# One item of the inverse split in two, and the gates' exponents listed as items of their own

## The chip, the cores and the metric

The kernel runs on one core of one Trainium2 chip. The metric is the device time of one execution in microseconds. The engines of the core are named as in the profile: PE (TensorE, matmuls), PEld (its weight loads), DVE (VectorE), ACT (ScalarE), POOL (GpSimd) and SP (SyncE, whose queue issues most DMAs). Each engine works through its own instructions in order and waits on semaphores for the others.

## The reference

Two layers of a hybrid block over 256 context and 256 latent tokens of width 1024, all in f32. Each layer norms and modulates its input, projects it, and feeds three mixers: a gated linear attention, a gated DeltaNet in both directions, and a latent attention. Their outputs are gated, projected, merged and projected again. What the change touches is the DeltaNet, and in it the inverse of a unit lower triangular matrix per chunk and head, and the sigmoid gates of the merge:

```python
l_strict = jnp.where(strict, jnp.einsum('bnthd,bnshd->bnhts', k_beta, k) * decay, 0.0)
t_inv = lax.linalg.triangular_solve(eye + l_strict, jnp.broadcast_to(eye, l_strict.shape),
                                    left_side=True, lower=True, unit_diagonal=True)
u = jnp.einsum('bnhts,bnshv->bnthv', t_inv, v_beta)
w = jnp.einsum('bnhts,bnshd->bnthd', t_inv, k_beta * jnp.exp(g_cum)[..., None])
...
def step(s, inp):
    w_n, u_n, qd_n, att_n, ke_n, d_n = inp
    v_new = u_n - jnp.einsum('bthd,bhdv->bthv', w_n, s)
    o_n = jnp.einsum('bthd,bhdv->bthv', qd_n, s) + jnp.einsum('bhts,bshv->bthv', att_n, v_new)
    s = s * d_n[..., None, None] + jnp.einsum('bshd,bshv->bhdv', ke_n, v_new)
...
def merge_branches(ya, yb, yc, gate_logits, w_branch, w_out):
    ys = jnp.einsum('btiw,iwd->btid', jnp.stack([ya, yb, yc], axis=2), w_branch)
    gates = jax.nn.sigmoid(gate_logits.reshape(B, T, N_BRANCH, D_MODEL))
    return jnp.einsum('btd,de->bte', jnp.sum(gates * ys, axis=2), w_out)
```

## The kernel before

The whole program is one list, made by `schedule()`. An entry is an item such as `("dw", l, g)`: a kind, the layer `l` (0 or 1) and further indices. Every engine walks the same list and for each item issues the instructions that are its part, so an item may have matmuls on PE, then a function on ACT and a product on DVE, with semaphores between. The order of the list is the order on each engine. The list is put together from shorter ones: `weave` merges several of them so that each progresses evenly by the sum of its items' loads (1.0 for most, 0.3 for a few light kinds), and `settle` at the end moves kinds by a fixed number of places (table `AHEAD`; for `gx` it is -4, four places later, for `dx6`, `dya` and `dy6` 3 and for `dyb` 2 places earlier; `dw` has no entry). An item more in one of the woven lists therefore also moves its neighbours. Long matmul groups are cut in quarter pieces (`("pc", ...)`), between which other items may stand. Eight PSUM banks and four slots of weights (`ring`) are handed out along the list; PE waits for a bank's readers and for its weights.

The DeltaNet's heads are taken in four groups of two (`g`). The items of a group:

- `dqkv`, `cv`, `dsilu`, `dsil2`, `dnq`, `dn`: projection, convolution, silu (three functions on ACT, L1471 to L1473, for `dsilu`, an exponent for `dsil2`, L1690) and norm of the next group's q, k, v.
- `d1`, `d2`, `dd`, `dt`: decays (an exponent on ACT, L1710), the products of keys, four copies of the diagonal blocks by ACT (L1723) and a small transpose by DVE (L2119), per token tile. SP then stores the blocks to DRAM.
- `sol`: POOL loads all blocks of 32 x 32 of the group (L1068), solves them, and lands the inverses in SBUF again (the last DMAs are issued on L1094).
- `dv`: DVE copies the landed blocks (L2140) and transposes them (L2143).
- `dw`: ACT sets the blocks in their places, four copies into `XN` (L1734) and eight into `bXT` (L1739), each with 32 partitions and 256 elements.
- `dx`, `dya`, `dyb`, `dx6`, `dy6`: PE joins the blocks to 64 and then 128; DVE takes `dx` (L2145), `dya` and `dx6` out of PSUM, ACT takes `dyb` (four copies, L1746), and both take `dy6` (L1751 on ACT). `dx6` reads `XN`, `dy6` and the scan read `bXT`.
- `d3`: transposed keys and values of a tile; ACT copies one half (L1716), DVE multiplies the other (L2127).
- `sk`, `sq`, `st`, `su`, `sa`: the four steps of the scan. `st` is copied by ACT (L1757) before `su` and `sa` may use it.

Gates come in the merge: `gate` (projection of a block of 128 columns, three functions on ACT, L1471 to L1473, and DVE's subtraction, which is the item with the mark `"v"`, L1934) and `ys` (projection of the branch). In `ys` ACT first takes the exponent of the gate (L1652), then DVE multiplies (L1948). For six blocks of the last layer the exponent is an item `gx` of its own already (L1646). The gates and `ys` pieces of branch 0 are woven as filling work around the inverses and scans; PE does the other matmuls of the list while the small chain runs.

Of the kernel before, what the change touches and what calls it, by code (L numbers as in the profile page):

```python
# [9 lines left out]
ACT = mybir.ActivationFunctionType  # L10
# [6 lines left out]
KT = D // P  # L17
# [155 lines left out]
def schedule():  # L173
# [31 lines left out]
    def merge(l, br):  # L205
        if keeps(("gate", l, br, 0)):
            out = [i for e in range(6, 8) for i in pieces(("gate", l, br, e)) + [("v", "gate", l, br, e)]]
            return out + [i for e in range(8) for i in pieces(("ys", l, br, e))]
        out = []
        for e in range(9):  # L210
# [3 lines left out]
            out += p[:2] + ([("v", "gate", l, br, e)] if e < 8 else []) + p[2:]  # L214
# [60 lines left out]
    def invert(l, g):  # L275

        return [(k, l, g) for k in ("dv", "dw", "dx", "dya", "dyb", "dx6", "dy6")]
# [85 lines left out]
    for l in range(DEPTH):  # L363
# [20 lines left out]
        if sums:  # L384
# [13 lines left out]
          "dv": "invert", "dw": "invert", "dx": "invert", "dya": "invert", "dyb": "invert", "dx6": "invert", "dy6": "invert",  # L398
# [4 lines left out]
         "dd": 0, "dt": 0, "sol": 0, "dv": 0, "dw": 0, "dg": 2}  # L403
# [61 lines left out]
def hybrid_block(nc, x, c, ctx_in, c_ctx, norm_w, ada_w, ada_b, w_in, gla_gate_w2, gla_gate_b, gla_norm_w,  # L465
# [55 lines left out]
    with ExitStack() as stack:  # L521
# [153 lines left out]
        def takes_part(it, who):  # L675
            return not (it[0] == "ys" and keeps(it) and who == "act")
# [77 lines left out]
        for key, its in phase_items.items():  # L754
            d = {}
            for it in its:
# [357 lines left out]
        def _(pe):  # L1114
# [10 lines left out]
            for it in plan:  # L1125
# [340 lines left out]
        def _(act):  # L1466
# [38 lines left out]
            for it in plan:  # L1505
# [135 lines left out]
                elif k == "gx":  # L1641
                    gi = ("gate",) + it[1:]
                    act.wait_ge(*done(gi, "dve"))
                    act.wait_ge(s_spill, 16 * (l + 1))
                    act.wait_ge(s_scaled, KT * (l + 1))
                    ins = nc.scalar.activation(yT[:, it[3], 0:LC], E1[:, zg_index[gi] % 2, LC:T], ACT.Exp)  # L1646
                elif k in ("z2", "ys"):

                    zi = ("z" if k == "z2" else "gate",) + it[1:]
                    act.wait_ge(*done(zi, "dve"))  # L1650
                    e = E1[:, zg_index[zi] % 2, (q0 if k == "ys" else 0):512]
# [675 lines left out]
```

## Time and profile before

| what | us |
|---|---|
| median of 3 runs | 2241.01 |
| lowest, highest | 2238.62, 2243.85 |
| profiled execution | 2241.74 |
| its span, first to last instruction | 2239.9 |
| PE busy | 2138.0 |
| DVE, ACT, POOL busy | 917.0, 846.1, 291.5 |

The page of the profile gives the busy time of every engine. A timeline row gives the start, the duration, the engine, the line, the operation with its operands and how many records were merged; in brackets stands the idle time in front and what ended it. A matmul in f32 has two records, a transpose through PE one.

### The profile page before, as it was taken

Reading aid. Unit: us, or ns where it says so; the run is one execution under the profiler, and the core shown is the slowest. Engines: PE = TensorE matmul, PEld = TensorE weight load, DVE = VectorE, ACT = ScalarE, POOL = GpSimd, SP = SyncE. Lnnn points to the kernel's source line nnn. Section 1 sums busy time; section 2 is a strip of 40 time slices with the busy share of each in tenths; the row PEclk is TensorE's granted clock in tenths of the full one; section 3 lists DMA queues with packets and bytes.
Section 4 is the critical chain, followed back from the end, with each engine's and each line's share of the span. In section 5 each row is a group of like instructions: output and inputs, shape, how many; then the busy total and the mean of one; then the engine's idle time right before and its main releaser. Section 6 shows DMA issues by size and latency. Waiting matters only on the chain. (4 is left out here: it accounts for less than half of the span.)

```text
span 2239.9 us, 31521 instructions
## 1 busy us (share of the span) xinstructions
PE 2138.0 (95%) x10970; PEld 1458.9 (65%) x10970; DVE 917.0 (41%) x2281; ACT 846.1 (38%) x2205; POOL 291.5 (13%) x623
## 2 busy tenths in 40 slices
PE   7999899999989999999999998999989979999998
PEld 4667576655555786555584445776666758877687
DVE  2023374657554325333331111136486654343321
ACT  2223263546343224444332102245455453244420
POOL 1000006061431000000000001000523532000000
PEclk9999999999999999999999999999999999999999
DMA  8324412221212122111321325221332222332333
GB/s 269 101 67 160 126 41 78 79 60 53 85 34 67 29 66 87 48 38 40 95 75 57 119 74 171 59 76 39 95 95 86 72 62 87 102 106 70 123 116 130
DMA packets 192444, 192.32 MB, mean 86 GB/s; under 512 B 28943, under 2 KB 186467, under 8 KB 191779
## 3 DMA queue, kind: packets, MB, share of 16 engines
q1 hardware_dynamic: 186048, 171.08, 24.7%
q0 software_dynamic: 4672, 18.89, 2.7%
q8 instruction: 93, 1.52, 0.3%
q10 hardware_dynamic: 1571, 0.34, 0.1%
q14 instruction: 60, 0.49, 0.1%
HBM read 180.78 MB, written 9.50 MB: 85 GB/s over the span
## 5 line engine op out<-in xcount | busy, mean ns | idle before, releaser
L1118 PE MATMUL bank<-hT,ring 128*128 128x512 f32 (+2 forms) x1856 | 721.1, 539 | 3.6 <-DVE hT L1882 2.1
L1118 PEld LDWEIGHTS bank<-hT,ring 128*128 128x128 f32 (+1 forms) x1856 | 333.1, 190 | 257.9 <-issue 240.5
L1118 PE MATMUL bank<-ring,hT 128*128 128x256 f32 (+2 forms) x2112 | 455.2, 371 | 12.6 <-DMA ring<-in_w_in_dram 12.6
L1118 PEld LDWEIGHTS bank<-ring,hT 128*128 128x128 f32 x2112 | 383.9, 192 | 77.2 <-issue 30.2
L1118 PE MATMUL bank<-WORK 128*128 128x128 f32 (+6 forms) x3056 | 393.0, 286 | 30.6 <-issue 8.7
L1118 PEld LDWEIGHTS bank<-WORK 128*128 128x128 f32 (+4 forms) x3056 | 320.9, 171 | 134.7 <-issue 117.1
L1118 PE MATMUL bank<-yT,ring 128*128 128x512 f32 (+1 forms) x768 | 268.7, 487 | 0.0
L1118 PEld LDWEIGHTS bank<-yT,ring 128*128 128x128 f32 x768 | 138.8, 190 | 83.7 <-issue 75.4
L1471 ACT ACTIVATE E<-bank 128x512 f32<-128x512 f32 (+1 forms) x84 | 44.9, 535 | 254.0 <-PE bank L1118 253.8
L2068 DVE SCALAR_TENSOR_TENSOR WORK<-WORK,CW 128x512 f32<-128x512 f32 (+1 forms) x192 | 139.0, 724 | 2.3
L1118 PE MATMUL bank<-ring,WORK 128*128 128x384 f32 (+1 forms) x272 | 108.4, 536 | 0.0
L1081 POOL TENSOR_TENSOR WORK<-WORK 128x126 f32<-128x126 f32 (+22 forms) x248 | 104.5, 421 | 19.4
L1106 POOL DMA_DIRECT2D yT<-xs x2 | 1.1, 548 | 809.4 <-DVE MT L1952 809.4
L1079 POOL TENSOR_TENSOR WORK<-WORK 128x126 f32<-128x126 f32 (+22 forms) x248 | 101.4, 409 | 19.5
L1483 ACT ACTIVATE WORK<-bank 128x128 f32<-128x128 f32 (+3 forms) x182 | 47.3, 272 | 134.3 <-PE bank L1118 134.1
L1118 PE MATMUL bank<-MT,ring 128*128 128x512 f32 (+1 forms) x256 | 83.9, 486 | 2.7 <-DVE MT L1952 2.7
L1121 PEld LDWEIGHTS bank<-K,WORK 128*128 128x128 f32 (+1 forms) x506 | 63.5, 143 | 31.0 <-issue 23.3
L1121 PE MATMUL bank<-K,WORK 128*128 128x128 f32 (+1 forms) x506 | 81.5, 279 | 0.0
L1118 PEld LDWEIGHTS bank<-ring,WORK 128*128 128x128 f32 x272 | 50.3, 190 | 37.9 <-issue 22.0
L1118 PEld LDWEIGHTS bank<-MT,ring 128*128 128x128 f32 x256 | 48.5, 190 | 37.2 <-issue 30.1
L1676 ACT ACTIVATE WORK<-bank 128x512 f32<-128x512 f32 (+1 forms) x48 | 26.9, 560 | 105.5 <-PE bank L1118 105.5
L1970 DVE SCALAR_TENSOR_TENSOR WORK<-bank,WORK 128x512 f32<-128x512 f32 x16 | 11.1, 692 | 126.9 <-ACT WORK L1473 126.9
(208 smaller groups left out, 2088.9 us busy)
## 6 DMA issues: line engine op xcount, KB each, us to landing
ring<-in_w_in_dram SPq DMA_DIRECT2D x92, 1024.0 KB, 5.4
ring<-in_w_branch_dram SPq DMA_DIRECT2D x24, 1024.0 KB, 5.1
ring<-in_ada_w_dram SPq DMA_DIRECT2D x18, 1024.0 KB, 5.6
ring<-in_w_out_dram SPq DMA_DIRECT2D x8, 1024.0 KB, 5.0
WORK<-in_ada_w_dram SPq DMA_DIRECT2D x6, 1024.0 KB, 12.3
ring<-in_mla_q_up_dram SPq DMA_DIRECT2D x8, 576.0 KB, 4.3
xs<-yT POOLq DMA_DIRECT2D x2, 2048.0 KB, 8.1
WORK<-LD POOLq DMA_DIRECT2D x16, 256.0 KB, 3.5
```

The costliest lines, as they stand in the source:

```text
L1079: link(pool, "pool", pool.tensor_tensor(t, a[:, j + 1:BASE, j:j + 1].broadcast_to([P, m, w]), y[:, j:j + 1, 0:w].broadcast_to([P, m, w]), ...
L1081: ins = pool.tensor_tensor(y[:, j + 1:BASE, 0:w], y[:, j + 1:BASE, 0:w], t, ALU.subtract)
L1106: pool.dma_start(yT[:, :, :], xs[l]).then_inc(s_back, 16)
L1118: return nc.tensor.matmul(o, a, b, start=start, stop=stop, skip_group_check=True)
L1121: return nc.tensor.transpose(o, a, ident)
L1471: link(act, "act", nc.scalar.activation(dst, src, ACT.Abs))
L1483: ins = nc.scalar.activation(MT2[:, c0:c0 + w], ps[:, c0:c0 + w], ACT.Square, accum_out=mS[:, at + i:at + i + 1])
L1676: ins = nc.scalar.activation(PAD[:, 2 * pj + a0:2 * pj + 2, 2:258], ps[:, a0 * LC:T].rearrange("p (s n) -> p s n", n=LC), ACT.Copy)
L1970: ins = V_.scalar_tensor_tensor(LA[:, tt, :], ps[:, :], 0.0, LT1, ALU.min, ALU.subtract)
L2068: ins = V_.scalar_tensor_tensor(acc, src, wv, acc, ALU.mult, ALU.add)
```

## The change

The eight copies into `bXT` leave `dw` and are a new item `dw2`, listed directly behind `dx`. `dx6` still waits for `dw`; `dy6` (on PE and DVE) waits for `dw2`, as do the next group's `dv` and the first readers of group 3's scan. The wait for the scan of the group before moves from `dw` to `dw2` and `dyb`.

Every gate gets an item `gx`, listed directly behind its `"v"` item, and takes its exponent there. `ys` has no part on ACT any more.

```diff
     def merge(l, br):
         if keeps(("gate", l, br, 0)):
-            out = [i for e in range(6, 8) for i in pieces(("gate", l, br, e)) + [("v", "gate", l, br, e)]]
+            out = [i for e in range(6, 8) for i in pieces(("gate", l, br, e)) + [("v", "gate", l, br, e), ("gx", l, br, e)]]
...
-            out += p[:2] + ([("v", "gate", l, br, e)] if e < 8 else []) + p[2:]
+            out += p[:2] + ([("v", "gate", l, br, e), ("gx", l, br, e)] if e < 8 else []) + p[2:]
...
     def invert(l, g):
-        return [(k, l, g) for k in ("dv", "dw", "dx", "dya", "dyb", "dx6", "dy6")]
+        return [(k, l, g) for k in ("dv", "dw", "dx", "dw2", "dya", "dyb", "dx6", "dy6")]
...
         def takes_part(it, who):
-            return not (it[0] == "ys" and keeps(it) and who == "act")
+            return not (it[0] == "ys" and who == "act")
...
                     pe.wait_ge(*done(("dx6", l, g), "dve"))
                     pe.wait_ge(*done(("dyb", l, g), "act"))
+                    pe.wait_ge(*done(("dw2", l, g), "act"))
...
                 elif k == "gx":
                     gi = ("gate",) + it[1:]
                     act.wait_ge(*done(gi, "dve"))
-                    act.wait_ge(s_spill, 16 * (l + 1))
-                    act.wait_ge(s_scaled, KT * (l + 1))
-                    ins = nc.scalar.activation(yT[:, it[3], 0:LC], E1[:, zg_index[gi] % 2, LC:T], ACT.Exp)
-                elif k in ("z2", "ys"):
+                    if keeps(gi):
+                        act.wait_ge(s_spill, 16 * (l + 1))
+                        act.wait_ge(s_scaled, KT * (l + 1))
+                        ins = nc.scalar.activation(yT[:, it[3], 0:LC], E1[:, zg_index[gi] % 2, LC:T], ACT.Exp)
+                    else:
+                        e = E1[:, zg_index[gi] % 2, q0:512]
+                        ins = nc.scalar.activation(e, e, ACT.Exp)
+                elif k == "z2":
...
                 elif k == "dw":
                     _, l, g = it
                     act.wait_ge(*done(("dv", l, g), "dve"))
+                    if g:
+                        act.wait_ge(*done(("dx6", l, g - 1), "pe"))
+                    for b in range(NBLK):
+                        half = slice(0, 2 * BASE) if b < 2 else slice(2 * BASE, 4 * BASE)
+                        ins = nc.scalar.activation(two_heads(XN)[blk(b), :, :, blk(b % 2)],
+                                             two_heads((LAND if b < 2 else LANDT)[:, :, half])[blk(b)], ACT.Copy)
+                elif k == "dw2":
+                    _, l, g = it
+                    act.wait_ge(*done(("dv", l, g), "dve"))
                     act.wait_ge(s_zero, 4 * l + 4)
                     if g:
                         scan_left(act, l, g - 1, NB - 1, "pe")
-                        act.wait_ge(*done(("dx6", l, g - 1), "pe"))
-                    for b in range(NBLK):
...
                     for b in range(NBLK):
                         for r in range(2):
...
                 elif k == "dyb":
                     _, l, g = it
+                    if g:
+                        scan_left(act, l, g - 1, NB - 1, "pe")
...
                     e = E1[:, zg_index[gi] % 2, q0:512]
+                    dve.wait_ge(*done(("gx",) + it[1:], "act"))
                     if keeps(it):
-                        dve.wait_ge(*done(("gx",) + it[1:], "act"))
                         e = yT[:, e8, 0:LC]
-                    else:
-                        dve.wait_ge(*done(it, "act"))
...
```

The order on ACT in layer 1 around the inverse of group 2, before. L1716 is a copy of `d3`, the four copies on L1734 and the eight on L1739 are `dw`, and L1652 is the exponent of a gate.

```order
L1716 ACTIVATE WORK<-bank 128x256
L1734 ACTIVATE O<-WORK 32x4x2x32 x2
L1734 ACTIVATE O<-O 32x4x2x32 x2
L1739 ACTIVATE WORK<-O 32x4x2x32
L1739 ACTIVATE WORK<-WORK 32x4x2x32
L1739 ACTIVATE WORK<-O 32x4x2x32
L1739 ACTIVATE WORK<-WORK 32x4x2x32
L1739 ACTIVATE WORK<-O 32x4x2x32
L1739 ACTIVATE WORK<-WORK 32x4x2x32
L1739 ACTIVATE WORK<-O 32x4x2x32
L1739 ACTIVATE WORK<-WORK 32x4x2x32
L1652 ACTIVATE E<-E 128x256
```

The same place of ACT in the changed kernel. L1714 is the exponent of `d1`, L1651 that of the gate, L1727 the copies of `dd`, L1720 `d3`, L1736 `dw` and L1747 the beginning of `dw2`.

```order
L1714 ACTIVATE SQ<-SQ 128x512 x2
L1651 ACTIVATE E<-E 128x256
L1727 ACTIVATE WORK<-SQ 32x128 x8
L1720 ACTIVATE WORK<-bank 128x256
L1736 ACTIVATE O<-WORK 32x4x2x32 x2
L1736 ACTIVATE O<-O 32x4x2x32 x2
L1720 ACTIVATE WORK<-bank 128x256
L1747 ACTIVATE WORK<-O 32x4x2x32
L1747 ACTIVATE WORK<-WORK 32x4x2x32
```

The exponent has moved from behind the twelve copies to before the last two `dd`, and one more `d3` copy has come between the four and the eight.

The order on ACT in layer 1 behind the inverse of group 1, before. L1471 to L1473 with `WORK` are the functions of `dsilu`, with `E` those of a gate; L1676 is a projection's copy, L1690 `dsil2`, and L1757 the copy of the first `st`.

```order
L1471 ACTIVATE WORK<-WORK 128x512
L1472 ACTIVATE WORK<-WORK 128x512
L1473 ACTIVATE WORK<-WORK 128x512
L1676 ACTIVATE WORK<-bank 128x256
L1690 ACTIVATE WORK<-WORK 128x512
L1471 ACTIVATE E<-bank 128x256
L1472 ACTIVATE E<-E 128x256
L1473 ACTIVATE E<-E 128x256
L1757 ACTIVATE WORK<-bank 128x512
L1471 ACTIVATE WORK<-WORK 128x512
L1472 ACTIVATE WORK<-WORK 128x512
L1473 ACTIVATE WORK<-WORK 128x512
```

The same place of ACT in the changed kernel, where every line number is a little higher (L1472 to L1474, L1680, L1694, and L1767 for `st`).

```order
L1472 ACTIVATE E<-bank 128x256
L1473 ACTIVATE E<-E 128x256
L1474 ACTIVATE E<-E 128x256
L1472 ACTIVATE WORK<-WORK 128x512
L1473 ACTIVATE WORK<-WORK 128x512
L1474 ACTIVATE WORK<-WORK 128x512
L1680 ACTIVATE WORK<-bank 128x256
L1694 ACTIVATE WORK<-WORK 128x512
L1472 ACTIVATE WORK<-WORK 128x512
L1473 ACTIVATE WORK<-WORK 128x512
L1474 ACTIVATE WORK<-WORK 128x512
L1767 ACTIVATE WORK<-bank 128x512
```

The gate's functions have moved ahead of the first `dsilu`, and the second `dsilu` ahead of the copy of `st`.

The order on PE in layer 1 from the last `dn` of group 3 (`RS`) to the first matmuls of `dx` of group 2 (32x32), before. `hT` rows are quarter pieces of gates, `yT` rows pieces of `ys`, `K,WORK` 128x128 x8 two `d1`, and `WORK` 128x128 rows are `d2`.

```order
L1118 MATMUL bank<-RS,ONES 128x512
L1118 MATMUL bank<-K,WORK 128x128 x8
L1118 MATMUL bank<-hT,ring 128x256 x2
L1118 MATMUL bank<-WORK 128x128 x4
L1118 MATMUL bank<-hT,ring 128x256 x2
L1118 MATMUL bank<-K,WORK 128x128 x8
L1118 MATMUL bank<-yT,ring 128x256 x2
L1118 MATMUL bank<-WORK 128x128 x8
L1118 MATMUL bank<-yT,ring 128x256 x4
L1121 MATMUL bank<-K,WORK 128x128 x4
L1118 MATMUL bank<-yT,ring 128x256 x2
L1118 MATMUL bank<-WORK 32x32 x2
```

The same place of PE in the changed kernel.

```order
L1118 MATMUL bank<-RS,ONES 128x512
L1118 MATMUL bank<-K,WORK 128x128 x8
L1118 MATMUL bank<-yT,ring 128x256 x2
L1118 MATMUL bank<-WORK 128x128 x4
L1118 MATMUL bank<-yT,ring 128x256 x2
L1118 MATMUL bank<-K,WORK 128x128 x8
L1118 MATMUL bank<-WORK 128x128 x8
L1118 MATMUL bank<-yT,ring 128x256 x4
L1118 MATMUL bank<-hT,ring 128x256 x2
L1121 MATMUL bank<-K,WORK 128x128 x4
L1118 MATMUL bank<-hT,ring 128x256 x2
L1118 MATMUL bank<-WORK 32x32 x2
```

The two gate pieces (`hT`) that stood behind the `dn` have gone ahead of it, into the scan of group 1, and two pieces of the next gate stand ahead of `dx` instead.

## Rows read from the trace of the kernel before

**Rows 1.** The page: the span, and busy time, share and instructions of each engine

```profile
span 2239.9 us, 31521 instructions
PE 2138.0 (95%) x10970; PEld 1458.9 (65%) x10970; DVE 917.0 (41%) x2281; ACT 846.1 (38%) x2205; POOL 291.5 (13%) x623
```

**Rows 2.** Waits of PE: total us, times, longest

```profile
PE bank L1118 <- DVE WORK L2145: 9.7, 4, 5.1
```

**Rows 3.** Timeline of PE, layer 1, group 2: start, us, operation, count [idle before]

```profile
1821.11 0.18 PE L1118 MATMUL bank<-WORK 32*32 32x32 f32 x1 [4.17 <-DVE O L2143]
...
1827.04 0.23 PE L1118 MATMUL bank<-WORK,O 32*32 32x32 f32 x1 [5.10 <-DVE WORK L2145]
...
1828.95 3.54 PE L1118 MATMUL bank<-hT,ring 128*128 128x256 f32 x8
...
1867.73 3.62 PE L1118 MATMUL bank<-hT,ring 128*128 128x256 f32 x16
```

**Rows 4.** Timelines of ACT and DVE at the same place

```profile
1825.63 0.42 ACT L1652 ACTIVATE E<-E 128x256 f32<-128x256 f32 x1
...
1826.13 0.42 DVE L1948 TENSOR_TENSOR MT<-bank,E 128x256 f32<-128x256 f32 x1 [4.54 <-issue]
1826.47 0.41 DVE L2145 COPY WORK<-bank 128x256 f32<-128x256 f32 x1
```

**Rows 5.** Timelines of DVE, POOL and PE: the solve of layer 1, group 3

```profile
1819.14 0.24 DVE L2119 STREAM_TRANSPOSE WORK<-WORK 128x64 f32<-128x64 f32 x1 [1.18 <-ACT WORK L1723]
...
1821.77 0.54 POOL L1068 DMA_DIRECT2D WORK<-LD  x1 [28.22 <-DMA LD<-WORK]
...
1869.33 0.43 DVE L2140 COPY WORK<-WORK 128x512 f32<-128x512 f32 x1 [1.88 <-DMA WORK<-XD]
...
1871.28 0.21 PE L1118 MATMUL bank<-WORK 32*32 32x32 f32 x1
```

**Rows 6.** Line L1739, copies of `dw`: ns least/median/most, first and last start

```profile
L1739 ACT ACTIVATE WORK<-O x32: 412/414/418, 435.5 to 1874.6; 32x256 f32<-32x256 f32 x32
```

**Rows 7.** Timelines of PE, DVE and ACT, layer 1, inverse and first scan step of group 1

```profile
1728.09 0.18 PE L1118 MATMUL bank<-WORK,O 32*32 32x32 f32 x1 [2.35 <-DVE WORK L2145]
...
1735.57 0.76 DVE L2127 TENSOR_TENSOR WORK<-bank,WORK 128x256 f32<-128x256 f32 x2 [0.22 <-ACT WORK L1716]
...
1737.99 1.52 ACT L1746 ACTIVATE WORK<-bank 32x256 f32<-32x256 f32 x4
...
1739.66 0.53 PE L1118 MATMUL bank<-WORK 64*64 64x64 f32 x11 [0.23 <-ACT WORK L1746]
...
1748.51 0.58 ACT L1757 ACTIVATE WORK<-bank 128x512 f32<-128x512 f32 x1
...
1749.19 1.13 PE L1118 MATMUL bank<-WORK 128*128 128x128 f32 x8 [1.23 <-issue]
```

**Rows 8.** Groups of ACT's instructions by line and shape: count, busy us, mean ns, idle before

```profile
L1472 ACT ACTIVATE WORK<-WORK 128x512 f32<-128x512 f32 x56 | 35.3, 630 | 1.8
```

**Rows 9.** Timelines of PE and DVE, layer 0

```profile
445.94 1.17 PE L1118 MATMUL bank<-WORK 64*64 64x64 f32 x32 [0.79 <-ACT WORK L1746]
...
642.71 0.23 PE L1118 MATMUL bank<-WORK 32*32 32x32 f32 x1 [4.42 <-DVE O L2143]
...
644.46 0.23 PE L1118 MATMUL bank<-WORK,O 32*32 32x32 f32 x1 [0.61 <-DVE WORK L2145]
...
676.10 2.02 PE L1118 MATMUL bank<-WORK 128*128 128x128 f32 x16 [1.27 <-DVE WORK L2163]
...
692.98 0.89 DVE L2143 STREAM_TRANSPOSE O<-WORK 128x128 f32<-128x128 f32 x4
...
697.38 0.21 PE L1118 MATMUL bank<-WORK 32*32 32x32 f32 x1
```

**Rows 10.** Busy time by stretch: us, engines (records), PE's granted clock, DMA share, GB/s

```profile
1822.00:1832.00 10.00, 4.96 (x44) 4.24 (x44) 2.35 (x6) 4.35 (x12) 6.09 (x14) 0.50 0.21 56
1400.00:1410.00 10.00, 10.00 (x48) 8.79 (x47) 0.69 (x1) 2.11 (x4) 0.00 (x0) 1.00 0.01 2
```

More of the change, by code:

```diff
@@ L397 @@
 FAMILY = {"d1": "head", "d2": "head", "dd": "head", "dt": "head", "d3": "head",
-          "dv": "invert", "dw": "invert", "dx": "invert", "dya": "invert", "dyb": "invert", "dx6": "invert", "dy6": "invert",
+          "dv": "invert", "dw": "invert", "dw2": "invert", "dx": "invert", "dya": "invert", "dyb": "invert", "dx6": "invert", "dy6": "invert",
           "sk": "scan", "sq": "scan", "st": "scan", "su": "scan", "sa": "scan"}
 NBANK = {"nx": 0, "nh": 0, "cv": 0, "dsilu": 0, "dsil2": 0, "dnq": 0, "osq": 0, "z2": 0, "gx": 0, "rstd": 0, "ge": 2, "mkv": 1,
-         "dd": 0, "dt": 0, "sol": 0, "dv": 0, "dw": 0, "dg": 2}
+         "dd": 0, "dt": 0, "sol": 0, "dv": 0, "dw": 0, "dw2": 0, "dg": 2}
 READERS = {"xin": ("act",), "par": ("act",), "mod": ("dve",), "modT": ("dve",), "norm": ("act",), "z": ("act", "dve"),
@@ L763, in hybrid_block @@
         NODVE = {"gx", "norm", "osq", "dqkv", "pc", "dnq", "xin", "gqk", "gv", "lr", "mp", "xout", "mkT",
-                 "dd", "sol", "dw", "dyb", "st"}
+                 "dd", "sol", "dw", "dw2", "dyb", "st"}
         POOLK = {"sol"}
@@ L768, in hybrid_block @@
                 continue
-            if k not in ("nx", "nh", "cv", "dsilu", "dsil2", "dnq", "osq", "z2", "gx", "rstd", "dd", "dt", "sol", "dv", "dw"):
+            if k not in ("nx", "nh", "cv", "dsilu", "dsil2", "dnq", "osq", "z2", "gx", "rstd", "dd", "dt", "sol", "dv", "dw", "dw2"):
                 parts["pe"].add(k)
@@ L1643, in _ @@
                     act.wait_ge(*done(gi, "dve"))
-                    act.wait_ge(s_spill, 16 * (l + 1))
-                    act.wait_ge(s_scaled, KT * (l + 1))
-                    ins = nc.scalar.activation(yT[:, it[3], 0:LC], E1[:, zg_index[gi] % 2, LC:T], ACT.Exp)
-                elif k in ("z2", "ys"):
-                    zi = ("z" if k == "z2" else "gate",) + it[1:]
+                    if keeps(gi):
[6 more added lines that the diff above has]
+                elif k == "z2":
+                    zi = ("z",) + it[1:]
                     act.wait_ge(*done(zi, "dve"))
-                    e = E1[:, zg_index[zi] % 2, (q0 if k == "ys" else 0):512]
+                    e = E1[:, zg_index[zi] % 2, :]
                     ins = nc.scalar.activation(e, e, ACT.Exp)
@@ L1730, in _ @@
                         scan_left(act, l, g - 1, NB - 1, "pe")
-                        act.wait_ge(*done(("dx6", l, g - 1), "pe"))
-                    for b in range(NBLK):
-                        half = slice(0, 2 * BASE) if b < 2 else slice(2 * BASE, 4 * BASE)
-                        nc.scalar.activation(two_heads(XN)[blk(b), :, :, blk(b % 2)],
-                                             two_heads((LAND if b < 2 else LANDT)[:, :, half])[blk(b)], ACT.Copy)
                     for b in range(NBLK):
@@ L2133, in _ @@
                         dve.wait_ge(*done(("dyb", l, g - 1), "pe"))
-                        dve.wait_ge(*done(("dw", l, g - 1), "act"))
+                        dve.wait_ge(*done(("dw2", l, g - 1), "act"))
                     else:
@@ L2153, in _ @@
                     _, l, g = it
-                    dve.wait_ge(*done(("dw", l, g), "act"))
+                    dve.wait_ge(*done(("dw2", l, g), "act"))
                     ins = V_.tensor_scalar(two_heads(bXT[:, :, 256:512])[CH:P, :, :, 0:CH],
@@ L2168, in _ @@
                         dve.wait_ge(*done(("dx6", l, g), "pe"))
-                        dve.wait_ge(*done(("dw", l, g), "act"))
+                        dve.wait_ge(*done(("dw2", l, g), "act"))
                     for tt in tiles(l):
@@ L2198, in _ @@
                         dve.wait_ge(*done(("dx6", l, g), "pe"))
-                        dve.wait_ge(*done(("dw", l, g), "act"))
+                        dve.wait_ge(*done(("dw2", l, g), "act"))
                     if n:
```

2 rows, old and new, of the table PHASE are left out of this document.

## The prediction

> **What bounds the kernel now.** I read the page first: TensorE (PE) is busy 2138.0 of 2239.9 us [rows 1], which leaves 102 us in which it stands still. With this change PE issues the same matmuls in another order, so only this idle time, and the clock that follows them, can move. Next the waits of PE: the longest that is no weight load is 9.7 us for DVE's copy of `dx` (L2145) [rows 2]. It belongs to the inverse of the delta rule, which runs eight times (two layers, four groups of heads). The timeline of PE then shows where they are worst: in layer 1, group 2, where PE stands still 4.17 us ahead of `dx` and 5.10 us ahead of `dya` [rows 3].
>
> The timelines of ACT and DVE tell why. ACT reaches the exponent of an old gate (L1652) only at 1825.63, behind the twelve copies of `dw`; DVE waits for it until 1826.13 and has `dx`'s copy queued behind, at 1826.47; PE's `dya` waits for that [rows 4]. The change removes exactly this queue.
>
> The third thing to read is what comes next. Group 3's inverse starts with a solve on POOL. Its input is complete when DVE has done the last small transpose of `dt` at 1819.14; POOL issues its loads at 1821.77; DVE gets the result at 1869.33 after 1.88 us in which it waited for the DMA; and PE's `dx` of group 3 starts at 1871.28 with no gap in front [rows 5]. That is 1869.33 - 1819.38 = 50 us of a chain in which PE has no part. `dv`'s copy takes 0.43 and its four transposes 0.89 (as in layer 0 [rows 9]), which ends at 1870.7, so PE arrived at most 0.5 us after it could have started.
>
> **Part 1, the exponents as items of their own.** No instruction is added: each exponent moves up in ACT's queue, ahead of `dw` in the case above. It waits for DVE's logarithm step only, which stands at least four items ahead, so I cost the move itself at 0. What it frees: `dya`'s wait of 5.10 us goes, and of the 4.17 us ahead of `dx` a part, since two quarter pieces more (0.9 us each: 16 records of four pieces took 3.62 us) now stand in front of it on PE [rows 3]. That would be up to 9.3 us, and with the clock more. I do not count it, because all of it lies between 1819.14 and 1871.28. PE would be early at `dx` of group 3 and wait there for the solve: the gain is at most the 0.5 us of slack. What is late next is the POOL chain, and its start decides.
>
> **Part 2, where the chain starts now.** The new items shift the order that is woven from the lists. Ahead of `dn` of group 3 in layer 1 PE now has two more quarter pieces of the gates (in the order, the gate pieces that stood behind the first `d1` of group 3 have gone ahead, and a `ys` piece stands there). Everything that leads to `dt` hangs on that `dn` (the wait ahead of the first `d2` is DVE's latency and stays), so the solve starts 2 x 0.9 = 1.8 us later. Bounds: 0, if DVE's own queue sets the time, and 1.9. I take 1.8, since PE has no gaps in the stretch before it.
>
> **Part 3, eight of the twelve copies as `dw2`.** The copies cost what they did: eight of 0.41 us, 3.3 us in all [rows 6]. `dx6` never was late for `dw` in a way that the waits show, so its earlier release is worth nothing. DVE's `d3` step of the next tile waited for an ACT copy behind the twelve; one such copy now passes, the next still stands behind all twelve and both `dd`. In layer 1, group 1, DVE waited for it until 1735.57 and starts there again at about the same time [rows 7]. But `dyb`'s copies now stand behind the second exponent of `d1` (0.63 plus the wait for DVE, some 0.9 us): they began at 1737.99 and will at 1738.9, so `dy6` goes from 1739.66 to about 1740.5. The 2.35 us wait at `dya` [rows 7] is thus not won, it moves to `dy6`, where PE will stand some 4 us.
>
> Then the first scan step of group 1. Its copy on ACT (L1757) ran at 1748.51, ahead of the second silu's three functions; PE's `su` followed at 1749.19 after 1.23 us [rows 7]. Now the gate's logarithm stands ahead of the first silu, and the second silu ahead of the copy. Three functions of 512 columns take 3 x 0.63 = 1.9 us [rows 8], three of 256 columns by estimate 1.2. So the copy starts at 1748.5 + 0.9 + 1.2 + 1.9 = 1752.5 and `su` at about 1753.0, with one piece (0.9) more behind PE than before: a loss of 1753.0 - 1749.2 - 0.9 = 2.9 us. Bounds: 0 (ACT has idle time that takes it all) and 3.5 (a step of the scan with a piece less between its matmuls as well). I take 2.9.
>
> By the Trainium skill (ScalarE: Activation LUTs, Rules for kernel authors) an ACTIVATE costs about 0.3 us and 0.83 ns for each element of a row, 0.51 us for a copy of 256. The rows have 0.41. By the page `dw2` would take 4.1 us, and what stands behind it would be 0.8 us later; the measured rows decide.
>
> **Part 4, layer 0.** In groups 0 and 1 `dy6` waited 0.79 us for `dyb`'s copies [rows 9]; by the same order as above it will be about 0.3 us later in each, measured against the work done: +0.6. In group 2 the exponent no longer stands between the `dd` copies: DVE and so `dv` come 0.5 us earlier at `dx`, whose wait was 4.42; a `d3` piece of 0.5 us now covers the 0.61 us ahead of `dya`: -1.1. In its scan a `ys` piece goes between a `sk` and its `st`, where 1.27 us were waited, and leaves another pair with less: -0.5 net. Here `dv` of the next group was done at 693.9 and PE came to its `dx` at 697.4 [rows 9], so this is kept. Sum: -1.0, from -3 to +1.
>
> **Part 5, the clock.** PE's granted clock in 1822 to 1832 is 0.50 (1.2 GHz), against 1.00 (2.4 GHz) in a stretch without gaps [rows 10]; it stayed low for 5 us after the wait ended at 1827.04, and four pieces of a gate, 16 records, cost 3.62 us at full clock while 8 records cost 3.54 there [rows 3]. Those slow microseconds lay ahead of `dx` of group 3, where they were hidden by the solve. Now the wait of some 9 us stands at `dx` itself, and slow time behind it is on the path: 5 us at half speed lose 2.5 us. Bounds: 0 and 3.4. I take 2.5.
>
> The Trainium skill (TensorE: Matmul & The Clock Gate, Part 1: The HAM clock gate) says that the clock gate passes half the pulses after the engine has been idle and all of them once it has been busy again. By that rule, the trace agrees, a wait that is only moved keeps its clock cost, and here exposes it.
>
> **The sum**, against the profiled execution's 2241.74 us (its span of 2239.9 and 1.8 around it): -1.0 (layer 0) + 2.9 + 1.8 - 0.4 (slack at `dx` of group 3) + 2.5 = +5.8, that is 2247.5. The profiled execution lay 0.7 above the median of the runs shown, 2241.01, so I predict 2246.8.
>
> **Rivals.**
> A. The reordering does not delay the start of the solve (parts 2 and 3 near 0), the gain is still lost at `dx` of group 3. For it: ACT and DVE have idle time in group 1. Against it: the order of ACT is the one shown above, in-order queues give nothing back. Then -1.0 - 0.4 + 2.5 = +1.1: 2242. No change.
> B. Faster. DVE's chain to `dt` comes earlier than I think, since the exponent and a gate's step left its way, or the solve was not last. The 9.3 us of waits and about 2.5 us of slow clock go: 2241 - 11.8 = 2229; with half of it, 2235. Against it: DVE's 1.88 us wait for the DMA [rows 5], which no earlier PE can shorten.
> C. Slower by more: the first steps of both scans in layer 1 fall behind the silu functions as in part 3, and the clock falls in two places on the path (after `dy6` of group 1 as well, 1.7 us), 2247 + 1.7 + 3.5 = 2252. It decides if `su` of group 1 waits over 3 us.
> D. The change does not do what it says, `dw2` running directly behind `dw`: excluded by the order, where a `d3` copy or both `dd` stand between.
>
> **Chances.** The forecast 0.42, A 0.30, B 0.14, C 0.14. A measurement of this kernel tells about 0.2% (4.5 us) from no change: B is the side of faster, A and a part of the forecast's lower half (0.06) are the same, the rest is slower. Faster 0.14, same 0.36, slower 0.50. The range for 8 in 10, from the half-gain of B to just over C: 2236 to 2253.
>
> **What would show it.** Right: in layer 1, group 2, no wait of 5 us at `dya`; instead a wait of 5 to 10 us of PE for `dv` at `dx` of group 3, with DVE idle for the DMA ahead of L2140's successor, and a clock of 0.5 behind it; `su` of group 1 later than its work by 2 to 3 us; the time from `dt` to `dv` still 50 us. Wrong: if `dx` of group 3 starts earlier than 1871 less what was gained in layer 0, the solve was not the bound; if it starts there with no wait in front, PE lost time I did not see. If PE's idle time falls by more than 5 us in sum, B holds.

## The result, and the profile after

The changed kernel takes 2246.45 us (median of 20 runs, 2241.17 to 2254.43), the kernel before 2241.77 (20 runs, 2238.4 to 2246.41). The ratio is 1.0025, with a 95% interval of 1.0015 to 1.0034: slower by a quarter of a per cent. The forecast was 2246.8, slower. The profiled execution of the changed kernel took 2244.56 us, 1.9 less than its median; that of before had 2241.74.

The first lines of the page of the changed kernel (they answer to [rows 1]):

```profile
span 2242.8 us, 31541 instructions
...
PE 2142.6 (96%) x10970; PEld 1463.8 (65%) x10970; DVE 916.5 (41%) x2281; ACT 846.3 (38%) x2205; POOL 291.4 (13%) x623
```

PE has the same 10970 matmuls. It stands still for 2242.8 - 2142.6 = 100.2 us, against 101.9, and its matmuls take 4.6 us longer. So in these two executions the idle time did not grow; it moved, and the clock behind it cost more.

PE's longest waits that are no weight load, from its table of waits (total us, times, longest); [rows 2] had 9.7 us for DVE's copy, now line 2153:

```profile
PE bank L1118 <- DVE O L2151: 12.7, 3, 4.4
...
PE bank L1118 <- DVE WORK L2120: 8.2, 4, 3.4
...
PE bank L1118 <- DVE WORK L2153: 2.3, 2, 1.6
```

The same table of the kernel before has, for `dv`'s transposes (L2143 there):

```profile
PE bank L1118 <- DVE O L2143: 8.6, 2, 4.4
```

The copy's 9.7 us are 2.3. In their place `dv`'s transposes (L2151) have grown from 8.6 to 12.7 us, and 8.2 us have come for the last product of `d2` (L2120), which was not in the table before. The timeline of PE in layer 1 shows where (start, us, operation, [idle before]); it answers to [rows 3], [rows 5] and [rows 7]:

```profile
1721.98 0.18 PE L1118 MATMUL bank<-WORK,O 32*32 32x32 f32 x1 [0.72 <-DVE WORK L2153]
...
1734.04 1.17 PE L1118 MATMUL bank<-WORK 64*64 64x64 f32 x32 [3.37 <-DVE WORK L2120]
...
1746.69 1.13 PE L1118 MATMUL bank<-WORK 128*128 128x128 f32 x8 [2.27 <-issue]
...
1803.32 1.02 PE L1118 MATMUL bank<-RS,ONES 128*128 128x512 f32 x2
...
1821.48 0.23 PE L1118 MATMUL bank<-WORK 32*32 32x32 f32 x1 [3.84 <-DVE O L2151]
...
1823.57 0.26 PE L1118 MATMUL bank<-WORK,O 32*32 32x32 f32 x1
...
1870.42 0.23 PE L1118 MATMUL bank<-WORK 32*32 32x32 f32 x1 [4.42 <-DVE O L2151]
```

These are, in order, `dya`, `dy6` and `su` of group 1, `dn` of group 3, `dx` and `dya` of group 2 and `dx` of group 3. `dya` of group 2 no longer waits at all (5.10 before). `dx` of group 3, which had no gap, waits 4.42 us. The reason stands in the timelines of three engines. ACT, whose exponent of the gate is gone from between `dw` (L1736) and what follows:

```profile
1822.22 0.84 ACT L1736 ACTIVATE O<-O 32x256 f32<-32x256 f32 x2
...
1824.09 0.42 ACT L1747 ACTIVATE WORK<-O 32x256 f32<-32x256 f32 x1
```

DVE:

```profile
1819.85 0.24 DVE L2127 STREAM_TRANSPOSE WORK<-WORK 128x64 f32<-128x64 f32 x1 [0.86 <-ACT WORK L1727]
...
1822.65 0.42 DVE L2153 COPY WORK<-bank 128x256 f32<-128x256 f32 x1 [0.68 <-PE bank L1118]
...
1868.91 0.43 DVE L2148 COPY WORK<-WORK 128x512 f32<-128x512 f32 x1 [7.15 <-DMA WORK<-XD]
```

POOL:

```profile
1822.47 0.55 POOL L1068 DMA_DIRECT2D WORK<-LD  x1 [35.02 <-DMA LD<-WORK]
...
1828.08 1.91 POOL L1072 TENSOR_TENSOR WORK<-WORK 128x1024 f32<-128x1024 f32 x1 [3.51 <-DMA WORK<-BD]
...
1863.83 2.32 POOL L1094 DMA_DIRECT2D WORK<-XD  x2 [2.44 <-DMA XD<-WORK]
```

DVE copies `dx` at 1822.65, with no exponent ahead of it. Then the solve: its input is complete at 1820.09 and DVE has the result at 1868.91. That is 48.8 us, with 7.15 us in which DVE waits for the DMA, against 50 and 1.88 [rows 5].

Both traces can be lined up at the same pieces of work. Changed minus before, of the start on PE: first `d2` of group 1 in layer 1, -4.91 us; `dn` of group 3, +0.70; `dx` of group 3, -0.87; first `z` after the delta rule, 1960.10 against 1958.22, +1.88. So from the first `d2` of group 1 to that `z` the changed kernel loses 6.79 us. Layer 0's stretch, from the last `dn` of its group 1 (423.54, 424.52) to the `z` behind its delta rule (819.06, 820.88), gains 0.84. The rest of the -4.91 has little to do with the delta rule: 1.0 us lies ahead of 424, and 3.1 us between the two delta rules, where PE has the same matmuls, for a part in another order. Nearly all of the 3.1 is clock. The kernel before had a mean granted clock of 0.83 in the ten microseconds around that `z` (820 to 830) and 0.57 in 1511 to 1519; the changed kernel had 1.00 (818 to 828) and 0.79 (1509 to 1517) at the same work. That is some 1.7 us of lost time less in each place, and it is chance of these two executions as far as the runs show.

### The profile page after: what moved, and what is told of

The parts are those of the page before. It is cut to its first block and busy times, and to the rows that moved or that the text cites. A ratio compares the mean times of both kernels' runs of the same rounds, so it can differ in the third digit from the quotient of the medians.

```text
span 2242.8 us, 31541 instructions
## 1 busy us (share of the span) xinstructions
PE 2142.6 (96%) x10970; PEld 1463.8 (65%) x10970; DVE 916.5 (41%) x2281; ACT 846.3 (38%) x2205; POOL 291.4 (13%) x623
## 5 line engine op out<-in xcount | busy, mean ns | idle before, releaser
L1118 PE MATMUL bank<-WORK 128*128 128x128 f32 (+6 forms) x3056 | 395.3, 287 | 40.6 <-DVE O L2151 12.7
L1472 ACT ACTIVATE E<-bank 128x512 f32<-128x512 f32 (+1 forms) x84 | 45.0, 535 | 228.3 <-PE bank L1118 228.0
L1680 ACT ACTIVATE WORK<-bank 128x512 f32<-128x512 f32 (+1 forms) x48 | 26.9, 561 | 103.1 <-PE bank L1118 103.1
## 6 DMA issues: line engine op xcount, KB each, us to landing
WORK<-in_ada_w_dram SPq DMA_DIRECT2D x6, 1024.0 KB, 12.7
```

The lines of the kernel that those rows point to most:

```text
L1118: return nc.tensor.matmul(o, a, b, start=start, stop=stop, skip_group_check=True)
L1472: link(act, "act", nc.scalar.activation(dst, src, ACT.Abs))
L1680: ins = nc.scalar.activation(PAD[:, 2 * pj + a0:2 * pj + 2, 2:258], ps[:, a0 * LC:T].rearrange("p (s n) -> p s n", n=LC), ACT.Copy)
```

## The experiments

Each ran beside the kernel before, whose median was 2241.71 beside `x1`, `x2`, `x3` and `x9`, 2241.06 beside `x4`, `x5`, `x10` and `x11`, and 2240.81 beside `x12` to `x15`. Ratios are to it, with the 95% interval. The changed kernel did not run again beside them, so against it the ratios are compared (it has 1.0025, 1.0015 to 1.0034) and not only the medians.

**One part alone.** `x1_gx_only` keeps the exponents as items and takes the split of `dw` back:

```
-        return [(k, l, g) for k in ("dv", "dw", "dx", "dw2", "dya", "dyb", "dx6", "dy6")]
+        return [(k, l, g) for k in ("dv", "dw", "dx", "dya", "dyb", "dx6", "dy6")]
```

> Only the exponents are items of their own; dw keeps its twelve copies. Theory S (the reordering delays the solve of layer 1, group 3, and its PE wait swallows what the inverse of group 2 gains): dn(1,3,3) stands behind the same two gate pieces more as in the changed kernel, and the gate's logarithm stands ahead of dsilu and of the first st copy in group 1, so su(1,1,0) waits over 2 us and dx of group 3 waits 3 to 5 us; 2244 to 2247. Theory F (the loss of the changed kernel comes from dw2, the gain from the exponents): no wait over 1 us at dx of group 3, 2235 to 2238.

Measured: 2251.65, ratio 1.0040 (1.0026 to 1.0055). `x2_dw2_only` keeps the split and takes the exponents back:

```
-            out += p[:2] + ([("v", "gate", l, br, e), ("gx", l, br, e)] if e < 8 else []) + p[2:]
+            out += p[:2] + ([("v", "gate", l, br, e)] if e < 8 else []) + p[2:]
```

> Only dw is split; the exponent stays in the ys item. It then stands behind four copies of dw, not twelve, so the 5.10 us wait at dya of layer 1, group 2 falls to about 1.8 us in this run too. Theory S: the order ahead of dn(1,3,3) is that of before, so the solve starts when it did, dx of group 3 has one piece less of PE work ahead of it (1.0 us) and waits 3 to 5 us, with slow clock behind it (2 to 3 us): 2242 to 2245. Theory F (waits won on PE count in full): 2236 to 2239; or, if dw2 itself costs (more copies behind dx, dy6 waits for it), 2246 or more with a wait at dy6 for ACT L17xx in every group.

Measured: 2251.84, ratio 1.0043 (1.0028 to 1.0059). Both medians are some 5 us above that of the whole change; by the ratios it is 3 to 4 us, and the intervals overlap a little. Both expectations missed the time. The waits that they named are there: at `dx` of group 3, 4.08 us in the first and 4.06 in the second; at `dya` of group 2, 1.49 in the second. What I had not seen is how far each new order upsets the groups ahead. PE in the first, at `su` of layer 1, group 1:

```profile
1755.49 1.83 PE L1118 MATMUL bank<-WORK 128*128 128x128 f32 x7 [4.42 <-issue]
```

ACT's copy for it, behind the logarithm and the silu, ran at 1754.81 and took 0.58. PE in the second, at `dy6` of layer 0, groups 0 and 1, where [rows 9] had 0.79:

```profile
445.42 1.17 PE L1118 MATMUL bank<-WORK 64*64 64x64 f32 x32 [2.97 <-DVE WORK L2119]
...
546.49 2.00 PE L1118 MATMUL bank<-WORK 64*64 64x64 f32 x32 [2.88 <-DVE WORK L2119]
```

So these two runs give no price for either part alone: each subset gives another woven order, and with it other waits. The next run holds the order fixed.

**The same items in the old order.** `x3_old_order` weaves the lists without the new items and puts them in afterwards:

```
+    for i in front + settle(s):
+        out.append(i)
+        if i[0] == "dx":
+            out.append(("dw2",) + i[1:])
+        if i[:2] == ("v", "gate") and not keeps(i[1:]):
+            out.append(("gx",) + i[2:])
```

> All items of the changed kernel, but every old item in the order of the kernel before (gx put directly behind its logarithm, dw2 directly behind dx, after all lists are woven). Theory S: PE does the same in the same order, dya's wait of 5.10 us in layer 1, group 2 goes, the solve starts at the same time as before, so dx of group 3 waits some 4.5 us instead and exposes 2 to 3 us of slow clock; group 1 loses nothing: 2242 to 2244.5. Theory W (the new items cost by themselves, their semaphores and waits on ACT and DVE): 2245 to 2248, as the changed kernel. Theory F (waits won count in full): 2233 to 2237.

Measured: 2244.10, ratio 1.0011 (1.0000 to 1.0021), inside the expectation of theory S. PE, at `dya` of group 2 and `dx` of group 3:

```profile
1823.93 0.23 PE L1125 MATMUL bank<-WORK,O 32*32 32x32 f32 x1 [0.61 <-DVE WORK L2160]
...
1870.89 0.18 PE L1125 MATMUL bank<-WORK 32*32 32x32 f32 x1 [3.30 <-DVE O L2158]
```

`dya`'s wait fell from 5.10 to 0.61 us and `dx` of group 3 waits 3.30. The pure change wins nothing and loses at most a little. Half of the 4.7 us of the real one, some 2.3 by the medians, would then be its order, but the two intervals (1.0000 to 1.0021 and 1.0015 to 1.0034) overlap, so this share is not shown. Theory W (the items cost by themselves) would have had this kernel at the changed one's 1.0025, which lies above its interval.

**The solve made shorter.** `x4_short_solve` (changed kernel) and `x5_before_short_solve` (kernel before) leave eight steps of one solve out:

```
                     for j in range(BASE - 1):
+                        if (l, g) == (1, 3) and 8 <= j < 16:
+                            continue
```

> The changed kernel, with eight of the 31 elimination steps of POOL's solve left out in layer 1, group 3 alone (steps 8 to 15; that part isn't computed). In the trace of the changed kernel these took 9.1 us (1836.92 to 1846.05). Theory S (the solve bounds dx of group 3): PE's wait of 4.42 us there goes, and the 2 to 3 us of slow clock behind it: 5 to 7 us less than the changed kernel, 2239.5 to 2241.5. Rival (another engine would release dx a little later, or the loss in the changed kernel lies in group 1 alone): under 2 us less, 2244.5 or more.

> The kernel before with the same eight steps of the solve left out in layer 1, group 3. Theory S: PE came to dx of group 3 at most 0.5 us behind the solve, so there is next to nothing to win: 2241 to 2242, within 1 us of before. Rival (a shorter solve helps any version, POOL's memory traffic or DMAs disturb the others): 2 us or more faster, 2239 or less.

Measured: 2242.89, ratio 1.0002 (0.9989 to 1.0015), and 2240.79, ratio 0.9995 (0.9985 to 1.0005). One of the eleven runs of `x5_before_short_solve` took 9737.42 us and is not in its ratio. The changed kernel loses 3.6 us of its 2246.45, the kernel before nothing that can be told. PE in `x4_short_solve`, at `dx` of group 3, and DVE there:

```profile
1869.01 2.75 PE L1120 MATMUL bank<-hT,ring 128*128 128x256 f32 x12
1871.69 0.21 PE L1120 MATMUL bank<-WORK 32*32 32x32 f32 x1
```

DVE, same kernel:

```profile
1867.45 0.43 DVE L2150 COPY WORK<-WORK 128x512 f32<-128x512 f32 x1
```

No gap on PE, no wait for the DMA on DVE. From `dya` of group 2 to the `z` behind the delta rule this trace takes 129.9 us (1829.09 to 1958.98), the changed kernel's 136.5 (1823.57 to 1960.10): 6.6 us, 4.42 of them the wait. The median moved by 3.6 only, below the expected 5 to 7; by the ratios (1.0025 to 1.0002) it is some 5 us. The gain is clear, its size is not.

**ACT's order in group 1.** `x9_st_first` moves one item:

```
+    s.remove(("st", 1, 1, 0))
+    s.insert(s.index(("dsil2", 1, 2, 4)), ("st", 1, 1, 0))
```

> The changed kernel with one item moved: the first st of layer 1, group 1 stands ahead of dsil2 and of the gate's logarithm, so that ACT copies it before them; PE's order is the same. Theory S: su(1,1,0) no longer waits 2.28 us but under 0.6, and everything behind it, the start of the solve too, comes 1.7 to 2.3 us earlier, up to 4.5 if the slow clock behind su(1,1,0) goes as well: 2242 to 2244.7. Rival (su is bound by DVE, or the silu that now comes later takes it back at a dn of group 2's keys): no change, 2246 to 2247.

Measured: 2242.91, ratio 1.0008 (0.9996 to 1.0019): 3.5 us less than the changed kernel, with one copy in another place of ACT's queue. The intervals overlap at their ends. ACT in the changed kernel, then in this one:

```profile
1745.47 0.63 ACT L1474 ACTIVATE WORK<-WORK 128x512 f32<-128x512 f32 x1
1746.01 0.58 ACT L1767 ACTIVATE WORK<-bank 128x512 f32<-128x512 f32 x1
```

`x9_st_first`:

```profile
1748.28 0.60 ACT L1770 ACTIVATE WORK<-bank 128x512 f32<-128x512 f32 x1 [0.47 <-PE bank L1121]
1748.78 0.62 ACT L1697 ACTIVATE WORK<-WORK 128x512 f32<-128x512 f32 x1
```

Above, the copy (L1767) comes behind the silu's third function and PE's `su` has waited 2.27 us for it. Below, ACT waits for PE and the silu comes behind; `su` has no gap, and the step behind it waits 1.26 us instead of 0.88.

`x14_dyb` adds one number to that, for `dy6`'s wait:

```
-'dyb': 2
+'dyb': 3
```

> As x9_st_first, and every dyb one item earlier (its advance raised from 2 to 3), so that in layer 1, group 1 ACT's copies for dyb stand ahead of the second exponent of d1 again, as in the kernel before. Theory S (the changed kernel's wait of 3.37 us at dy6 of group 1 comes from that order): the wait falls to under 1 us, everything behind it is 2.5 to 3 us earlier, the solve too: 2239 to 2241 against 2242.9. Rival (ACT has to wait for PE's dyb anyway, or the d1 exponent that now comes later holds up d2): within 1 us of 2242.9.

Measured: 2241.18, ratio 1.0003 (0.9994 to 1.0011). The median lies 0.2 us above the range expected, and by the interval it can't be told from `x9_st_first`. The step named did only a part: `dy6` waits 2.14 us instead of 3.37, not under 1. ACT there:

```profile
1728.87 0.40 ACT L1750 ACTIVATE WORK<-WORK 32x256 f32<-32x256 f32 x1
1729.29 0.38 ACT L1723 ACTIVATE WORK<-bank 128x256 f32<-128x256 f32 x1
1731.65 0.63 ACT L1717 ACTIVATE SQ<-SQ 128x512 f32<-128x512 f32 x1 [1.97 <-DVE SQ L2109]
1732.18 1.52 ACT L1759 ACTIVATE WORK<-bank 32x256 f32<-32x256 f32 x4
```

Behind the eight copies of `dw2` (L1750) stands the copy for `d3` (L1723); DVE needs it, and only then reaches the squares (L2109) for which ACT's exponent (L1717) waits 1.97 us, and `dyb`'s copies (L1759) behind it. So the order of `dyb` is 1.2 us of `dy6`'s wait in group 1, and the rest stands behind `dw2` ahead of `d3`'s copy. That second part is read from the chain of waits; no run moves that copy.

**Starting the solve earlier.** Four kernels move fill items (pieces of gates and `ys`) of layer 1 from group 1 to group 2, so that PE reaches `dn` of group 3 with less work:

```
+            if l == 1 and g == 1:
+                upto -= 8
             mine, at = fill[at:upto], upto
```

`x10_best` is the old order with eight items moved and `st` first, `x12_shift9` the same with nine; `x11_after_shift_st` is the changed kernel with eight moved and `st` first, `x13_shift3` with three; `x15_all` is `x13_shift3` with `dyb` earlier.

> The order of before with the new items (as x3_old_order), eight fill items of layer 1 moved from group 1 to group 2, and the first st of group 1 ahead of dsil2. PE has 6.2 us less work ahead of dn(1,3,3) and as much more between it and dx of group 3. Theory S: the solve starts 4 to 6 us earlier, the wait of 3.30 us at dx of group 3 and the slow clock behind it go, so the waits won in group 2 count at last; group 1 with less to cover its waits gives 1 to 2 us back: 2237 to 2240.5. Rival (group 1's inverse and scan need this cover: waits at dy6, su and st grow by as much as is won): 2243 to 2247.

> The changed kernel with the first st of group 1 ahead of dsil2 (as x9_st_first) and eight fill items of layer 1 moved from group 1 to group 2: 4.1 us less work of PE ahead of dn(1,3,3) than before, 6.2 less than in the changed kernel. Theory S: against x9_st_first (2242.9) the wait of 3.98 us at dx of group 3 and its slow clock go, less 1 to 2 us for lost cover in group 1: 2237.5 to 2241. Rival (the cover is needed): 2243 to 2247.

Measured: 2244.05, ratio 1.0012 (1.0002 to 1.0022), and 2245.10, ratio 1.0015 (1.0006 to 1.0025). Both missed. POOL in `x10_best`, and the DMA issues of 1818 to 1828 there (KB each, median us to landing):

```profile
1818.61 0.54 POOL L1079 DMA_DIRECT2D WORK<-LD  x1 [23.90 <-DMA LD<-WORK]
...
1827.09 1.91 POOL L1083 TENSOR_TENSOR WORK<-WORK 128x1024 f32<-128x1024 f32 x1 [6.38 <-DMA WORK<-BD]
```

The DMA:

```profile
q1 hardware_dynamic: 1040, 1.05, 34.5%
...
WORK<-LD POOLq DMA_DIRECT2D x2, 256.0 KB, 5.3
```

The loads are issued 3.2 us earlier than before (1821.77 [rows 5]), but the first multiply starts at 1827.09, where it had started at 1827.07. The 3.2 us went to the DMA: a weight load of 1.05 MB ran in the same microseconds, and the solve's input took 5.3 us. The moved pieces had carried with them the moment at which a weight slot comes free: SP issued that load at 1817.18, where the kernel before had issued one at 1809.50.

> As x10_best with nine fill items moved instead of eight. PE's work ahead of dn(1,3,3) is the same, but the last gate piece of branch 0, column block 1, whose end frees a slot for a 1 MB weight load, now stands behind dya of group 2, not ahead of dx: about 4 us later. In x10_best that load ran beside the solve's input load (256 KB, 5.3 us to landing against 3.6 before, and POOL waited 6.38 us against 3.20). Theory C (the collision took the 3 us that the earlier start had won): POOL's wait ahead of its first multiply falls back to 3 to 3.6 us, dx of group 3 comes 3 us earlier and waits under 3 us: 2239 to 2242 against x10_best's 2244.05. Rival (the load is long for another reason, or the cover lost in group 1 is what counts): 2243 to 2246.

Measured: 2242.26, ratio 1.0012 (1.0002 to 1.0022). POOL:

```profile
1816.19 0.54 POOL L1079 DMA_DIRECT2D WORK<-LD  x1 [23.61 <-DMA LD<-WORK]
...
1821.64 1.91 POOL L1083 TENSOR_TENSOR WORK<-WORK 128x1024 f32<-128x1024 f32 x1 [3.33 <-DMA WORK<-BD]
...
1860.57 2.32 POOL L1105 DMA_DIRECT2D WORK<-XD  x2 [5.51 <-DMA XD<-WORK]
```

With the load out of the way (issued at 1822.38) POOL waits 3.33 us for the input again: theory C is right in its mechanism. In time nothing was won, for the ratio is that of `x10_best`. Now the result's store waits 5.51 us instead of 2.44, beside another weight load, and PE still stands 3.29 us at `dx` of group 3.

> As x9_st_first with three fill items of layer 1 moved from group 1 to group 2: PE has 3.1 us less work ahead of dn(1,3,3), and the weight load's slot is freed some 4 us of work ahead of the solve's input, so the two should meet little. Theory S: the wait of 3.98 us at dx of group 3 falls to about 1, with less slow clock behind it: 2238.5 to 2241.5 against x9_st_first's 2242.9. Rival: the weight load meets the solve's load here too (over 5 us to landing), 2242 to 2244.5.

> The changed kernel with the three corrections together: first st of group 1 ahead of dsil2, dyb one item earlier, three fill items of layer 1 moved from group 1 to group 2. Theory S: the gains of x13_shift3 and x14_dyb add, less 1 us: 2235.5 to 2239, faster than the kernel before (2241.4) by 0.1 to 0.25%. Rival (a moved wait is paid at the next bound, DVE in group 1): 2240 to 2243.

Measured: 2242.52, ratio 1.0003 (0.9990 to 1.0015), and 2240.56, ratio 0.9995 (0.9986 to 1.0004). Both missed the range of their theory S. `x13_shift3` did what it should on POOL (3.10 and 2.73 us at the two transfers) and its wait at `dx` of group 3 is 2.37; its runs spread from 2235.86 to 2248.45. `x15_all` met a weight load at the store again:

```profile
1860.85 2.32 POOL L1099 DMA_DIRECT2D WORK<-XD  x2 [4.98 <-DMA XD<-WORK]
```

It has the lowest median of all: 5.9 us less than the changed kernel's 2246.45, and the same as the kernel before, since its interval holds 1. No version beat the kernel before.

## Why the prediction was right, and where not

**The bound.** The step on which it rested, that everything won in group 2 lies between the start of the solve and `dx` of group 3, was right, and is shown: in all eleven kernels with at least one of the new items and a full solve (all but x4 and x5) PE waits at `dx` of group 3, from 2.37 us in `x13_shift3` to 7.87 in `x11_after_shift_st`, and shortening the solve removes the wait in the changed kernel and moves nothing in the one before. Forecast wait 5 to 10 us, measured 4.42; chain 50, measured 48.8.

**Where the chain starts.** Forecast: `su` +2.9 and two pieces +1.8, so 4.7 us later than its work. Measured at `dn` of group 3: 0.70 + 4.91 = 5.6. The pieces are right: PE has eight records, two pieces, more ahead of that `dn`, 1.8 us by the forecast's price. `su` is mis-sized. Against its work it was 1.5 us late (1746.69 - 1749.19 + 4.91 - 0.9 for the piece in front), not 2.9. ACT's copy for it was to start 4.0 us later and started 2.4 later (1746.01 + 4.91 against 1748.51), and two of the three addends were wrong. The gate's three functions (1.2 us) were counted although they stood ahead of that copy before, too:

```profile
1747.34 0.37 ACT L1471 ACTIVATE E<-bank 128x256 f32<-128x256 f32 x1
```

And 0.9 us were added for `dyb`'s copies, which came 0.8 us earlier than before against the work (1732.27 + 4.91 against 1737.99), since the `dd` copies now stand ahead of `dw2`. ACT in the changed kernel did not run its functions one behind another either; it waited 0.91 us for PE and 1.42 for DVE in this stretch, where it had waited 0.66 before:

```profile
1744.15 0.63 ACT L1472 ACTIVATE WORK<-WORK 128x512 f32<-128x512 f32 x1 [1.42 <-DVE WORK L2076]
```

What the forecast left out here is slow clock. Busy time and PE's granted clock of both kernels, before first (us, then PE, PEld, DVE, ACT, POOL, clock, DMA, GB/s):

```profile
1728.00:1736.00 8.00, 7.91 (x156) 7.24 (x156) 3.39 (x10) 7.24 (x22) 0.00 (x0) 0.79 0.03 6
1746.00:1754.00 8.00, 5.89 (x39) 5.08 (x38) 6.35 (x14) 4.45 (x10) 2.27 (x5) 1.00 0.31 78
```

The changed kernel:

```profile
1734.00:1742.00 8.00, 7.96 (x60) 6.94 (x61) 6.33 (x14) 6.60 (x17) 1.12 (x3) 0.79 0.11 18
1746.00:1754.00 8.00, 6.43 (x29) 5.67 (x30) 2.93 (x7) 0.89 (x3) 6.55 (x16) 0.79 0.00 0
...
1870.00:1880.00 10.00, 9.58 (x125) 7.94 (x126) 4.02 (x12) 6.43 (x17) 0.00 (x0) 0.73 0.05 13
```

The changed kernel has a mean clock of 0.79 behind the waits at `dy6` and at `su` of group 1. The first of them is rival C's second place, but it is no new cost: the kernel before had 0.79 in 1728 to 1736, behind its wait of 2.35 us at `dya`. New is the one behind `su`, 0.21 x 8 = 1.7 us of work. The 5.6 us are then 1.5 for `su`, 1.8 for the pieces, 1.7 for this clock and 0.6 that stays unassigned. `x9_st_first` bears on it: taking away 2.3 us of wait gave 3.5 by the medians.

**`dy6` of group 1.** Forecast: at about 1740.5 with a wait of some 4 us. Measured 3.37, at 1734.04, which against the lead of 4.91 us is 1738.95. The wait did move there from `dya` (2.35 to 0.72), but I named the second exponent of `d1` as its cause; by `x14_dyb` the order of these two is 1.2 us of it, and the larger part stands behind `d3`'s copy, behind `dw2`.

**The chain from `dn` to `dx` of group 3.** Forecast -0.4, the slack at `dx`. Measured -1.6 (from +0.70 to -0.87). The slack gave its 0.4; most of the rest is a transfer that the prediction took as fixed. DMA issues of 1854 to 1871, the landing of the inverses, before and in the changed kernel (KB each, median us to landing):

```profile
WORK<-XD POOLq DMA_DIRECT2D x2, 128.0 KB, 5.4
```

The changed kernel:

```profile
WORK<-XD POOLq DMA_DIRECT2D x2, 128.0 KB, 3.8
```

Before, SP issued a weight load of 1 MB in the same microseconds:

```profile
1861.36 0.37 SPq L1002 DMA_DIRECT2D ring<-in_w_in_dram  x1
```

In the changed kernel the load at that place of the trace was issued at 1853.24. POOL issued these transfers at 1862.88 and 1863.83, and DVE had them 6.45 and 5.08 us later. So the chain's 48.8 us instead of 50 are no faster solve. The changed order moved a weight load out of the way of its last transfer, and gained 1.4 us by it. The two kernels with the short solve met a load there as well (4.7 and 5.7 us to landing); all the others, without a load there, have 3.8 or 3.9. No run moves that load alone.

**Layer 0.** Forecast -1.0, measured -0.84. That they agree is partly chance: behind the same wait of 1.91 us at `dn` of group 1 the changed kernel had a mean clock of 0.72 for six microseconds (423 to 429) and the kernel before 1.00 (424 to 430), which is 1.7 us. Without it the gain would be some 2.5.

**The clock behind `dx` of group 3.** Forecast +2.5. From `dx` of group 3 to `z` the difference grows from -0.87 to +1.88, which is 2.75; `su` and `st` of group 3 have 1.4 us of new small waits in it (0.51 and 0.88), of which 0.44 stood elsewhere before, so the clock's own part is nearer 1.8. Over many runs I can't show it: the mean granted clock was 0.9814 in the 20 runs of the changed kernel and 0.9815 in 26 runs of before. What the traces show as slow clock and what the medians show as 4.7 us may not be the same microseconds; this stays open.

**The sum.** For layer 1 the terms made 2.9 + 1.8 - 0.4 + 2.5 = 6.8, and 6.79 was measured between the first `d2` of group 1 and `z`: 5.61 up to `dn` of group 3, -1.57 from there to `dx`, +2.75 behind it. So close a match is luck in good part. `su` was 1.4 us too high, slow clock of 1.7 us in group 1 was left out, and the 1.4 us that the last transfer gave back were not foreseen. The whole was then lower in the profiled execution by the microseconds by which it led before, and right in the median, where these terms can't be told apart.

**Rivals.** A (no delay of the solve) is excluded by the +5.6. B (the solve is not the bound) by x3 and x4. D by the order. C described group 1 rightly in part (slow clock behind `dy6`, but `su` waited 2.27 us, not over 3), and its price was too high.

## What to carry to other kernels

Before counting a removed wait as a gain, look for a chain on other engines that starts ahead of the wait and ends behind it without passing through it. Here a solve of 49 us on POOL did, and the waits won beside it turned into a wait at its end. When items are added to a woven or planned order, compare the whole order first, and count only what newly stands ahead of an instruction: the gate's functions stood there before, and cost the forecast 1.2 us. By the medians 3.5 of the 4.7 us could be had back by moving one copy ahead of a silu in ACT's queue. And a piece of work that is moved takes the transfers with it that its end sets off, to the good (1.4 us at the end of the solve here) as to the bad (3 us at its start in `x10_best`).

## What the runs showed of the hardware that I had not expected

- The solve's 256 KB load took 3.6 us to land alone (kernel before) and 5.3 us beside a 1 MB weight load (`x10_best`); its 256 KB store 2.4 us alone (`x9_st_first`) and 5.5 us beside one (`x12_shift9`); its last two transfers of 128 KB 3.8 us alone (changed kernel) and 5.4 us beside one (kernel before). Which of them is hit changes with one matmul group's place.
- The same kernel spreads with the granted clock. Of 20 runs of the changed kernel the two with 0.978 had spans of 2250.7 and 2252.6 us, the three with 0.984 2239.4 to 2240.3. One wait is followed by slow microseconds in one execution and not in another. `dy6` of layer 1, group 0, waits 2.38 us both in the changed kernel and in `x9_st_first`, whose order is the same there. The 20 records behind it took 4.58 us in the first and 6.27 in the second, and the mean clock granted over ten microseconds (1651 to 1661, 1656 to 1666) was 1.00 (2.4 GHz throughout) and 0.83. PE in the changed kernel, then in `x9_st_first`:

```profile
1651.77 1.17 PE L1118 MATMUL bank<-WORK 64*64 64x64 f32 x32 [2.38 <-DVE WORK L2120]
1652.87 4.58 PE L1118 MATMUL bank<-hT,ring 128*128 128x256 f32 x20
```

The second:

```profile
1656.30 1.17 PE L1121 MATMUL bank<-WORK 64*64 64x64 f32 x32 [2.38 <-DVE WORK L2123]
1657.40 6.27 PE L1121 MATMUL bank<-hT,ring 128*128 128x256 f32 x20
```

This is why one profile is not enough to price a microsecond of clock, and why the medians above need their intervals.
